# Weight splits, yb splits and the turned state rows placed earlier in a decoder layer's step from the input projections to the branches

## The reference

```
h = rmsnorm(x, norm1_g) * (1 + sc1) + sh1
u_in, gate_c, gate_b, q, k, v, g_conv, g_attn = split_projection(h @ w_in)
conv_y, conv_state = short_conv(gate_c * u_in, conv_w, conv_past)
y_conv = (gate_b * conv_y) @ w_conv_out
...
attn_o, kv_state = attn_fn(q, k, v)
y_attn = attn_o.astype(x.dtype) @ w_attn_out
mixed = (jax.nn.sigmoid(g_conv) * y_conv + jax.nn.sigmoid(g_attn) * y_attn) @ w_o
x = x + gt1 * mixed
h2 = rmsnorm(x, norm2_g) * (1 + sc2) + sh2
x = x + gt2 * hier_moe(h2, w_rg, b_rg, w_re, b_re, w1, w3, w2)
```

## Time and profile before

| | us |
|---|---|
| median of 3 runs | 1140.19 (1140.02 to 1143.3) |
| the profiled execution's own time | 1138.12 |
| its span, first to last instruction | 1136.3 |
| PE busy | 1092.4 (96%) |
| VectorE busy | 553.2 (49%) |
| ScalarE busy | 358.9 (32%) |
| mean granted TensorE clock | 0.993 of full speed |

### The profile page before, as it was taken

The page is one execution under the profiler, slowest core; times in us unless marked ns, Lnnn a source line. Parts: engine busy times, 40 slices in busy tenths (PEclk is TensorE's granted clock), DMA queues, the critical chain, the costliest instruction groups (busy, mean ns, idle before and its releaser), DMA issues.

```text
span 1136.3 us, 28815 instructions
## 1 busy us (share of the span) xinstructions
PE 1092.4 (96%) x12103; PEld 940.8 (83%) x12103; DVE 553.2 (49%) x1221; ACT 358.9 (32%) x655; POOL 181.9 (16%) x245
## 2 busy tenths in 40 slices
PE   4899999999999999999989999999999999999995
PEld 3799999999999998888759999999956777777751
DVE  1845566565655655445344434445575333323337
ACT  6424233332333333233134444442341111111122
POOL 0334233233331200000000000000001111111114
PEclk9999999999999999999998999999999999999998
DMA  9979989989967756645988778629677999999995
GB/s 351 352 224 365 368 302 357 349 303 354 387 229 274 237 208 214 214 170 202 383 330 300 269 282 308 235 80 328 266 303 288 397 422 423 422 423 424 424 356 204
DMA packets 164622, 350.19 MB, mean 308 GB/s; under 512 B 11595, under 2 KB 116219, under 8 KB 149998
## 3 DMA queue, kind: packets, MB, share of 16 engines
q1 hardware_dynamic: 151902, 325.06, 77.7%
q0 software_dynamic: 5808, 16.05, 4.1%
q10 hardware_dynamic: 6832, 7.93, 2.0%
HBM read 321.95 MB, written 115.14 MB: 385 GB/s over the span
## 4 chain that ended last, share of the span: by engine, by line
PE 86%; DVE 5%; DMA 4%; ACT 2%; issue 2%; SPq 0%; POOL 0%; DVEq 0%; ACTq 0%; POOLq 0%
PE psum L959 50%; PE psum L1307 12%; PE psum L1319 6%; PE psum L1034 3%; DMA e<-in_w_dram 2%; PE psum L1020 2%; PE psum L1009 2%; PE psum L1000 2%; PE psum L1056 2%; PE psum L903 1%; PE psum L1083 1%; DMA y_rows<-yq 1%; PE psum L980 1%; DMA sttok<-in_state_conv_dram 1%; PE psum L1286 1%
## 5 line engine op out<-in xcount | busy, mean ns | idle before, releaser
L959 PE MATMUL psum<-hHi,whi 128*128 128x272 f32 x1216 | 358.8, 295 | 2.7 <-DVE hLo L1751 1.9
L959 PE MATMUL psum<-hLo,whi 128*128 128x272 f32 x1216 | 351.3, 289 | 0.0
L959 PE MATMUL psum<-hHi,wlo 128*128 128x272 f32 x1216 | 349.8, 288 | 0.0
L959 PEld LDWEIGHTS psum<-hHi,whi 128*128 128x128 f32 x1216 | 229.2, 188 | 15.4 <-issue 9.9
L959 PEld LDWEIGHTS psum<-hHi,wlo 128*128 128x128 f32 x1216 | 229.3, 189 | 0.0
L959 PEld LDWEIGHTS psum<-hLo,whi 128*128 128x128 f32 x1216 | 228.6, 188 | 0.0
L1307 PE MATMUL psum<-e,xs 128*32 128x256 f32 x3072 | 169.1, 379 | 0.0
L1703 DVE TENSOR_TENSOR wlo<-wraw,whi 128x1024 fp32r<-128x1024 f32 x100 | 132.5, 1328 | 73.4 <-ACT whi L1450 72.7
L1307 PEld LDWEIGHTS psum<-e,xs 128*32 128x32 f32 x3072 | 116.9, 110 | 48.5 <-issue 0.5
L1450 ACT ACTIVATE whi<-wraw 128x1024 fp32r<-128x1024 f32 x100 | 104.8, 1052 | 24.8 <-PE psum L959 24.8
L2495 POOL DMA_INDIRECT xg<-x_tok,piece x45 | 42.7, 949 | 434.4 <-DVE piece L2203 249.2
(11 more groups left out here) (372 smaller groups left out, 1555.4 us busy)
## 6 DMA issues: line engine op xcount, KB each, us to landing
e<-in_w_dram SPq DMA_DIRECT2D x96, 1024.0 KB, 15.6
wraw<-in_w_in_dram SPq DMA_DIRECT2D x76, 512.0 KB, 6.4
out_dram<-in_cache_k_dram SPq DMA_DIRECT2D x32, 1022.0 KB, 9.8
out_dram<-in_cache_v_dram SPq DMA_DIRECT2D x32, 1022.0 KB, 7.9
adar<-in_w_ada_dram SPq DMA_DIRECT2D x36, 512.0 KB, 7.2
kvr<-in_cache_k_dram SPq DMA_DIRECT2D x8, 2048.0 KB, 8.4
kvr<-in_cache_v_dram SPq DMA_DIRECT2D x8, 2048.0 KB, 11.4
out_dram<-in_cache_k_dram SPq DMA_DIRECT2D x8, 1016.0 KB, 9.4
```

What stands on the lines that cost most here:

```text
L959: mm = pe.matmul(psum[:, t, 0:HALF], w[:, slot, k, :], x[:, k, cols], start=(k == 0 and n == 0), stop=(k == k_n - 1 and n == 2))
```

## The change

Three moves, with no arithmetic changed:

1. ScalarE's and VectorE's splits of pieces 60, 61 and 62 are made within the loop, at G = 114, 116 and 118, as those of all pieces before them, and not after it.
2. `ybHi` of the channel blocks 0 to 2 (`YB_EARLY` = 3) is made by ScalarE at G = 117, and their `ybLo` by VectorE at the end of G = 118. The other five are made right after the loop, on VectorE ahead of slots 28 to 31 and no longer within them.
3. PE turns `last2` ahead of the second O slot (slot 31), and not after it.

```
-            for i in range(2 * C0 - DEC_G0, len(dec_slots)):
+            for i in range(2 * C0 - DEC_G0, len(dec_slots) - 1):
                 decode(i)
             pe.wait_ge(cu_done, 2 * KC)
             for k in range(KC):
                 mm = pe.transpose(psum[0:18, 6 + k // 4, ...], last2[:, k, :], ident[:, :])
             mm.then_inc(lt_pe, 1)
+            decode(len(dec_slots) - 1)
...
                 if t == 0:
-                    if m + LEAD < C0:
-                        split_hi_at(m + LEAD)
+                    split_hi_at(m + LEAD)
...
+                if G == 2 * C0 - 3:
+                    act.wait_ge(yb_done, 2 * (KC - 1))
+                    for n in range(YB_EARLY):
+                        act.activation(ybHi[:, n, :], yb[:, n, :], ACT.Copy).then_inc(yo_hi, 1)
-            for m in range(C0, C0 + LEAD):
-                split_hi_at(m)
             act.wait_ge(yb_done, 2 * KC)
-            for n in range(KC):
+            for n in range(YB_EARLY, KC):
                 act.activation(ybHi[:, n, :], yb[:, n, :], ACT.Copy).then_inc(yo_hi, 1)
...
+            def yb_lo(n):
+                dve.wait_ge(yo_hi, n + 1)
+                dve.tensor_tensor(ybLo[:, n, :], yb[:, n, :], ybHi[:, n, :].bitcast(F32),
+                                  ALU.subtract).then_inc(yo_lo, 1)
...
-                if t == 0 and m + LEAD < C0:
+                if t == 0:
                     split_lo((m + LEAD) % RING, m + LEAD + 1)
...
+                if G == 2 * C0 - 2:
+                    for n in range(YB_EARLY):
+                        yb_lo(n)
-            for m in range(C0, C0 + LEAD):
-                split_lo(m % RING, m + 1)
+            for n in range(YB_EARLY, KC):
+                yb_lo(n)
             for i in range(2 * C0 - DEC_G0, len(dec_slots)):
                 decode(i)
-                for n in range(KC):
-                    if n % 4 == i - (2 * C0 - DEC_G0):
-                        dve.wait_ge(yo_hi, n + 1)
-                        dve.tensor_tensor(ybLo[:, n, :], ...).then_inc(yo_lo, 1)
```

More of the change, by code:

```diff
@@ L78 @@
 ROWS_G = 2 * 39
+YB_EARLY = 3
 UNITS = TILES
@@ L227, in _build @@
     toks_at -= toks_at % 32
-    assert masks_at <= toks_at
+    assert masks_at <= toks_at and toks_at + YB_EARLY * NT * 4 <= rope_at
     zrow = Region(top - 2048 - 64)("zrow", [P, D // 2])
@@ L1984, in _ @@
                         dve.tensor_tensor(yb[:, f, cols], gb[:, n, :], yv[:, cols], ALU.mult).then_inc(yb_done, 1)
-            for m in range(C0, C0 + LEAD):
-                split_lo(m % RING, m + 1)
+                if G == 2 * C0 - 2:
[3 more added lines that the diff above has]
+                yb_lo(n)
             for i in range(2 * C0 - DEC_G0, len(dec_slots)):
                 decode(i)
-                for n in range(KC):
-                    if n % 4 == i - (2 * C0 - DEC_G0):
-                        dve.wait_ge(yo_hi, n + 1)
-                        dve.tensor_tensor(ybLo[:, n, :], yb[:, n, :], ybHi[:, n, :].bitcast(F32),
-                                          ALU.subtract).then_inc(yo_lo, 1)
             dve.wait_ge(yo_hi, KC + 1)
```

## The result

The changed kernel takes 1134.2 us in the median of 6 runs (1132.05 to 1135.05), the kernel before 1141.56 in 6 runs (1140.02 to 1144.44). The ratio is 0.993, with a 95% interval of 0.9919 to 0.9942: 0.7% faster, 7.4 us between the medians. The forecast was 1132.9 us, 7.33 less than the 1140.19 of the first three runs of before.

A forecast was written before the change was run, and what follows sets the result against it. It took PE, busy 96%, as the bound, with a 4.38 us idle stretch and half clock behind it to recover. 5.66 + 1.67 = 7.33 us, 1140.19 - 7.33 = 1132.9 us; range 1130.5 to 1136.3 (8 in 10).

The forecast's parts named there:

- What stood ahead of the branches: After the loop, five ybLo and the osm copy precede the O slot; first branch matmul 5.66 us earlier.
- Loop entry: Before the first branch matmul: 0.45 us after the releasing instruction, kept whole, though 0 to 0.45 was possible.
- The clock: First 15 branch matmuls at full instead of half clock: 1.67 us given back if the clock stays up.
- The clock rival: Clock falls all the same after the V slots: gain only 5.0 us, 1135.2 us; chance 10%.
- Moved work: Splits, ybHi and ybLo moved beside the projections cost 0.
- The cover for the last half of yb: VectorE's queue before yb's last half keeps 0.8 us to spare; each microsecond beyond costs one.
- bank 0: ScalarE frees it at 599.5, PE's second branch piece needs it at 600.71: 1.2 us to spare.
- SyncE's queue: Three shift_v3 and three weight loads issue by about 589, behind the cache load; cost 0.
- The rival of the late cache tile: Third V slot's cache tile lands late through shared DMA, V slot ends 13.4 us later: 1148 us; chance 6%.
- Downstream: Everything after the branches is released by PE, so the 7.33 us arrive whole at the end.
- The sum: 5.66 us from earlier branches plus 1.67 us from the clock give 7.33 us; median forecast 1132.9 us.

The follow-up runs named there:

- Experiments 1: Changed kernel with the splits of pieces 60 to 62 put after the loop again; ratio 0.9974 to the kernel before.
- experiment 2: Changed kernel with all eight ybHi after the loop and ybLo in slots 28 to 31, as before; ratio 0.9978 to the kernel before.
- 4: Kernel before with only the turning of last2 moved ahead of the second O slot; ratio 1.0016 to the kernel before.
- experiment 5: Kernel before with five unread matmuls added on PE ahead of the second O slot; ratio 0.998 to the kernel before.
- 3: Changed kernel with last2 turned after the O slot again; ratio 0.9951 to the kernel before.
- 6: Changed kernel with VectorE's last ybLo moved behind the osm copy, ahead of the oT copies; ratio 0.9922 to the kernel before.
- two replicas of before: Kernel before, unchanged, profiled twice more on a third chip; spans 1140.8 and 1138.9 us.
- first replica: Kernel before, unchanged, first of its two further profiles; span 1140.8 us.
- experiment 7: Changed kernel with three unread VectorE subtractions added, one before each early ybLo at G = 118; ratio 0.993 to the kernel before.
- Both replicas: Changed kernel, unchanged, profiled twice more on a third chip; spans 1130.9 and 1130.5 us.

## Why the prediction was right, by its own steps

**What stood ahead of the branches.** Right, and nearly to the number. After the last projection half the forecast had the last `ybLo` ending at 4.92 us and `osm` at 5.64; they ended at 4.89 and 5.62. Experiments 1 and 2 show what each of the two queue moves adds. Without part 1, A is 9.86, without part 2 it is 10.02, against 6.58 with both and 12.60 before: either lack costs more than half of the place, and each of them also leaves a hole behind which the clock falls, so of the kernels with moves only those with both get the clock's share.

**Loop entry.** This is the term that was mis-sized. I kept the 0.45 us before the first branch matmul whole. None of it was left: the first branch matmul started 0.91 us after the O slot did, where 0.81 for the O slot and 0.45 behind it were forecast, and A came out at 6.58 instead of 6.94. Where PE had to wait for a `ybLo` at this place, in experiments 2, 4 and 5, 0.44 to 0.45 us passed between the end of that `ybLo` and the matmul; where it did not wait (3 and 6, and the changed kernel), nothing did.

**The clock.** Forecast 1.67 us, measured 1.60 between the two first profiles (B less A, 179.70 and 178.10); experiment 5 measured 1.57 with nothing else changed. The cause (PE's hole) is shown by that experiment. That the size came out so near is in part luck: the two replicas of before put it at 2.0 (180.10 and 180.07), since the clock falls and rises elsewhere in them. So is the forecast's reading that the clock fell only after the idle stretch: in the first replica it fell within it. The clock rival did not happen in the changed kernel, where the clock stayed at 1.00 behind a hole of 0.27 us. But experiment 2 had half clock behind holes shorter than I had thought harmful.

**Moved work.** The cover for the last half of yb was forecast as 0.8 us. VectorE idled 0.85 before it, and experiment 7 spent it and paid the rest. For bank 0 the forecast was 1.2 us to spare. ScalarE's copy of it ended at 602.13 and PE's second piece began at 602.84, so 0.7; PE didn't wait.

**SyncE's queue.** The rival of the late cache tile did not happen. The load was issued at 587.01, landed in 5.0 us (5.3 before), and PE had no wait ahead of the third V slot. One thing in this step was wrong, though nothing hung on it: the copies and weight loads behind it were not out within 4 us. SyncE's timeline of the changed kernel:

```profile
588.68 0.41 SPq L795 DMA_DIRECT2D wraw<-in_w_conv_out_dram  x1
589.37 0.54 SPq L787 DMA_DIRECT2D out_dram<-in_cache_v_dram  x1
590.20 1.32 SPq L795 DMA_DIRECT2D wraw<-in_w_in_dram  x1
591.79 2.83 SPq L787 DMA_DIRECT2D out_dram<-in_cache_v_dram  x1
594.81 0.89 SPq L795 DMA_DIRECT2D wraw<-in_w_attn_out_dram  x1
595.97 0.71 SPq L787 DMA_DIRECT2D out_dram<-in_cache_v_dram  x1
```

In the kernel before, the six of these instructions from 590.54 on took 0.40 to 0.74 us each; the third and the fourth of them:

```profile
592.05 0.40 SPq L794 DMA_DIRECT2D wraw<-in_w_in_dram  x1
592.73 0.54 SPq L786 DMA_DIRECT2D out_dram<-in_cache_v_dram  x1
```

In the changed kernel the same two took 1.32 and 2.83 us, and the last of the six ended at 596.7. The first of them started no closer together than before (0.69 and 0.83 us apart, 0.68 and 0.83 before). What differs is that they follow the cache load and its copy without the pause of 4.6 us that lay there before (585.95 to 590.54). Both replicas show it too (1.59 and 2.84, 1.66 and 2.64 us). Why they take longer, no run shows. Nothing waited for them here.

**Downstream.** The gain passes to the end but for some tenths, which the scatter leaves open. The load of experts' weights on the chain took 26.45 us in the first profile of before and 27.45 in that of after, which looks like a return of 1.0 us; with the replicas (26.52 and 27.46 before, 26.94 and 27.34 after) it is within the scatter. On the second chip the stages behind the run took 384 to 387 us instead of 356 to 358, which is where its 2.6% lie (why is not known), and the kernels with all three parts still came out at 0.9922 and 0.993.

**The sum.** 5.66 + 1.67 = 7.33 forecast; 6.02 + 1.60 = 7.62 between the two first profiles; 7.9 over three profiles of each. The forecast median missed by 1.3 us because the median of before was 1141.56 over six runs, not 1140.19; the difference was nearly right. The term most off was the loop entry, by 0.36 us together with the O slot. Three small sums of the forecast don't come out as written and moved nothing: 4.47 - 7 x 0.55 is 0.62 and not 0.64, bank 0 would by its own terms be free at 599.4 and not at 599.5, and the late cache tile would have held the V slot for 13.6 us and not 13.4.

## What to carry to other kernels

At a seam between two stages, read the chain from the last matmul of the one to the first of the other, and ask of each link whether it needs the last data or only stands behind something that does; the three weight splits needed none of it. Price an idle stretch of PE with the matmuls at half clock behind it, which here added a fifth to a quarter of the gain, and read the granted clock behind every hole that an edit leaves: one of 2.36 us (with one of 1.19 ahead of it) was followed by half clock, one of 1.60 was not. Judge such an edit by distances between two events near it: B came out at 184.68 us in three executions of the changed kernel, while the end of the projections scattered by over 3 us between executions of the same kernel.

## What was not expected of the hardware

- Two holes of PE of 1.19 and 2.36 us, with an O slot of 1.08 us between them, were followed by half clock (0.50 from 599.6 to 603.0), as was one of 3.46 us; single holes of 1.25 and 1.60 us were not. No run has a single hole between 1.60 and 3.46 us. Part 3 alone, with holes of 3.40 and 2.36, paid for the clock in full.
- The kernel before has a scatter of 0.9 us of its own in B (192.30, 193.17, 192.32), and the clock falls at a different place in each; the changed kernel, whose clock doesn't fall there, has none that shows (184.68 three times).
- Six instructions of SyncE's queue that issue DMA took 0.40 to 0.74 us when a pause of 4.6 us lay ahead of them; without the pause, two of the six took 1.32 and 2.83 us.
